# State-space build moved from the first feed-forward into the mixing stage, and that feed-forward's up products as seven block products

## The reference, cut to what matters

```python
# first block, token mixer: the mixing stage
y_hy = hyena_branch(hy_cols, p) @ p['hy_proj']                  # 512 -> 1024
g_hy, g_rw = jnp.split(jax.nn.sigmoid(gate_cols), 2, axis=-1)   # gate_cols = h @ w_in[:, gates], 1024 -> 2048
mixed = (g_hy * y_hy + g_rw * (y_rw @ p['rw_proj'])) @ p['w_out']

# second block, feed-forward (run twice, layers 0 and 1)
up = h @ w_up                                                   # 1024 -> 5632
up = causal_conv(up, conv_w, width=3) + conv_b
val, gate = jnp.split(up, 2, axis=-1)
y = (jax.nn.silu(gate) * val) @ w_down                          # 2816 -> 1024

# second block, S5 mixer, between the two feed-forwards
x[t] = A_bar * x[t-1] + B_bar @ u[t];  y[t] = Re(C @ x[t]) + d * u[t]   # 64 groups, 64 complex states, 16 channels
```

## Time and profile before

| what | us |
|---|---|
| median of 3 runs | 3600.9 (3598.59 to 3601.1) |
| the profiled execution | 3596.73 |
| its span, first to last instruction | 3594.9 |
| TensorE busy in the span | 3275.0 (91%) |
| VectorE, ScalarE, GpSimd busy | 1454.7 (40%), 621.7 (17%), 8.5 (0%) |
| mixing, first to last product | 851.0 to 1017.8 |
| first feed-forward, up products, then down products | 2503.2 to 2808.4, to 2945.8 |
| second feed-forward, up products, then down products | 3189.3 to 3444.9, to 3583.1 |

### The profile page before, as it was taken

How to read it: one execution, slowest core, us unless ns; L and a number is a source line. 1 busy time by engine, 2 the same in 40 slices (tenths; PEclk the granted TensorE clock), 3 DMA queues, 4 the chain that set the end, 5 groups by cost and what they waited for, 6 DMA issues and landing times. The chain is left out here.

```text
span 3594.9 us, 49905 instructions
## 1 busy us (share of the span) xinstructions
PE 3275.0 (91%) x21661; PEld 1745.5 (49%) x21661; DVE 1454.7 (40%) x2603; ACT 621.7 (17%) x1237; POOL 8.5 (0%) x40
## 2 busy tenths in 40 slices
PE   6978899898997988898989899999999976999998
PEld 3557787444444333333333343455444434468853
DVE  2255666444013000000001135652666674157776
ACT  2033332110011000000000122151221003031200
POOL 0000000000000000000000000000000000000000
PEclk8989999899997999999999999999999997999999
DMA  6134435311226999999999821102333554222233
GB/s 237 58 105 164 166 130 183 114 59 47 82 77 269 430 430 430 430 431 427 426 425 430 368 75 47 61 10 65 135 129 130 169 179 188 71 70 71 94 135 129
DMA packets 202974, 689.83 MB, mean 192 GB/s; under 512 B 31240, under 2 KB 96252, under 8 KB 176517
## 3 DMA queue, kind: packets, MB, share of 16 engines
q1 hardware_dynamic: 201768, 686.28, 49.1%
q10 hardware_dynamic: 989, 0.36, 0.0%
HBM read 661.94 MB, written 22.31 MB: 190 GB/s over the span
## 5 line engine op out<-in xcount | busy, mean ns | idle before, releaser
L2086 PE MATMUL banks<-weight_ring,xe_T 128*64 128x512 f32 x1312 | 296.7, 599 | 41.2 <-DMA weight_ring<-in_exp_w 38.9
L2859 PE MATMUL banks<-h_T,weight_ring 128*128 128x512 f32 x704 | 306.5, 594 | 2.2 <-PEq L91 2.2
L2859 PEld LDWEIGHTS banks<-h_T,weight_ring 128*128 128x128 f32 x704 | 132.2, 190 | 163.2 <-issue 163.1
L2086 PEld LDWEIGHTS banks<-weight_ring,xe_T 128*64 128x64 f32 x1312 | 91.0, 137 | 234.3 <-issue 160.8
L2102 PE MATMUL banks<-weight_ring,hid_T 128*64 128x512 f32 x656 | 146.8, 596 | 10.6 <-DMA weight_ring<-in_exp_w 10.6
L2422 PE MATMUL banks<-h_T,weight_ring 128*128 128x512 f32 x320 | 142.1, 597 | 0.0
L2086 PE MATMUL banks<-h_T,xe_T 128*64 128x512 f32 x464 | 105.4, 596 | 18.2 <-DMA h_T<-in_exp_w 18.2
L1735 PE MATMUL banks<-h_T,weight_ring 128*128 128x512 f32 x256 | 112.9, 600 | 3.9 <-PEq L91 3.9
L3787 PE MATMUL banks<-weight_ring,h_T 128*128 128x512 f32 x256 | 112.9, 603 | 2.6 <-PEq L91 2.6
L3152 DVE SCALAR_TENSOR_TENSOR conv<-banks,cols,conv 128x511 f32<-128x511 f32 (+1 forms) x96 | 71.9, 749 | 100.5 <-ACT conv L2999 97.9
L2249 DVE TENSOR_TENSOR hid<-silu,banks 128x1024 f32<-128x1024 f32 x16 | 19.5, 1221 | 222.2 <-issue 179.4
(11 more groups left out here) (667 smaller groups left out, 5227.8 us busy)
## 6 DMA issues: line engine op xcount, KB each, us to landing
weight_ring<-in_exp_w SPq DMA_DIRECT2D x123, 2048.0 KB, 15.7
h_T<-in_exp_w SPq DMA_DIRECT2D x41, 2048.0 KB, 15.7
weight_ring<-in_ada_w SPq DMA_DIRECT2D x24, 2048.0 KB, 7.9
weight_ring<-in_ffn_w_up SPq DMA_DIRECT2D x44, 1024.0 KB, 7.2
weight_ring<-in_ffn_w_down SPq DMA_DIRECT2D x20, 2048.0 KB, 7.7
expert_out<-in_exp_w SPq DMA_DIRECT2D x19, 2048.0 KB, 19.4
weight_ring<-in_mod_w SPq DMA_DIRECT2D x12, 2048.0 KB, 8.4
spare<-in_exp_w SPq DMA_DIRECT2D x9, 2048.0 KB, 20.9
```

The costliest lines, as they stand in the source:

```text
L2086: mm = pe.matmul(k.ps[64 * half:64 * half + 64, 2 * c + b % 2, :], R.rows[:, e // 2 % 2, kt, (e % 2) * CAP:(e % 2 + 1) * CAP], w[:, r, 512 ...
L2859: mm = pe.matmul(k.ps[:, b + c, :], w[:, c, kt, m * P:m * P + P], hT[:, kt, :], start=kt == 0, stop=kt == 7)
```

## The change

`S5Build` is opened around `mix_branches` instead of `conv_ffn`. The mixing loop is cut into 24 slots of 8 matmuls (for each tile: one gate product, the other, both branch products), so that the build's pieces can stand after single slots; the gates take banks 0 to 3, the branch products banks 4 and 5 (one set instead of two), the build banks 6 and 7. A build step now has two slots; `dve_inputs` of step i stands one step further ahead, with two buffers for the input powers and for the fractions, and the wait for the stored tables has gone from `dve_inputs` to `dve_outputs`. The `used` count for the branch weights is now raised by VectorE. At the stage's end SP stores the taps as they are in a new DRAM tensor and waits for it; in the first feed-forward's up products `scatter_taps` scatters them from there, 8 DMAs after each of 8 chunks. The first feed-forward takes the form of the second.

```diff
+        self.s5_tap_rows = nc.dram_tensor("s5_tap_rows", (P, 8, P), F32, kind="Internal").ap()
...
-def mix_branches(k, hT, hy, rw, mixed):
+def mix_branches(k, hT, hy, rw, mixed, side):
 
     nc = k.nc
+    pair = k.ps[:, 6:8, :]
+
+    SLOTS_IN, STEPS = 3 * DT, 7
+    turn_at = {STEPS + 2 * i: i for i in range(8)}
+    taps_at = {STEPS + 2 * i + 1: i for i in range(8)}
+    gate_bank = lambda i: 2 * (i % 2)
+    loaded_by = (2, 2, 3, 4, 4, 5, 6, 6)
     with sbuf(nc, "gates", [P, 2, 2, L], F32) as gates, \
-            stage(nc, "products", "gated", "linked", "mixed_done") as (block, products, gated, linked, mixed_done):
+            stage(nc, "gate_products", "products", "gated", "linked", "mixed_done", *S5Build.SEMS) as \
+            (block, gate_products, products, gated, linked, mixed_done, *side_sems):
+        side.sem = dict(zip(S5Build.SEMS, side_sems))
+
         @block.sync
         def _(sync):
+            side.sync_start(sync)
+            k.ring.load_ahead(sync, 1)
+            side.sync_blank(sync)
+            for i in range(8):
+                k.ring.load_ahead(sync, loaded_by[i])
+                side.sync_store(sync, i)
             k.ring.load_ahead(sync, 8)
+            side.sync_end(sync)
 
         @block.tensor
         def _(pe):
-            for i in range(DT):
-                j, m, b = i // 2, i % 2, 4 * (i % 2)
-                if m == 0:
-                    k.ring.wait(pe, 2 * j)
+            for s in range(SLOTS_IN):
+                i, part = s // 3, s % 3
+                j, m = i // 2, i % 2
                 wg = k.ring.chunk(2 * j).rearrange("p (c k n) -> p c k n", c=2, k=8)
                 wp = k.ring.chunk(2 * j + 1)[:, 0:2048].rearrange("p (c k n) -> p c k n", c=2, k=4)
-                if i >= 2:
-                    pe.wait_ge(mixed_done, i - 1)
-                for c in range(2):
+                if part < 2:
+                    if m == 0 and part == 0:
+                        k.ring.wait(pe, 2 * j)
+                    if i >= 2 and part == 0:
+                        pe.wait_ge(gated, i - 1)
                     for kt in range(8):
-                        mm = pe.matmul(k.ps[:, b + c, :], wg[:, c, kt, m * P:m * P + P], hT[:, kt, 0:L], start=kt == 0, stop=kt == 7)
-                if m:
-                    mm.then_inc(k.ring.used, 1)
+                        mm = pe.matmul(k.ps[:, gate_bank(i) + part, :], wg[:, part, kt, m * P:m * P + P], hT[:, kt, 0:L], start=kt == 0, stop=kt == 7)
+                    if part:
+                        mm.then_inc(gate_products, 1)
                 else:
-                    k.ring.wait(pe, 2 * j + 1)
-                for c, src in ((0, hy), (1, rw)):
-                    for kt in range(4):
-                        mm = pe.matmul(k.ps[:, b + 2 + c, :], wp[:, c, kt, m * P:m * P + P], src[:, kt, :],
-                                       start=kt == 0, stop=kt == 3)
-                mm.then_inc(products, 1)
+                    if m == 0:
+                        k.ring.wait(pe, 2 * j + 1)
+                    if i:
+                        pe.wait_ge(mixed_done, i)
+                    for c, left in ((0, hy), (1, rw)):
+                        for kt in range(4):
+                            mm = pe.matmul(k.ps[:, 4 + c, :], wp[:, c, kt, m * P:m * P + P], left[:, kt, :], start=kt == 0, stop=kt == 3)
+                    mm.then_inc(products, 1)
+                if s == 2:
+                    side.pe_c(pe, pair)
+                if s == 3:
+                    side.pe_cols(pe, pair)
+                if s in turn_at:
+                    side.pe_turn(pe, turn_at[s], pair)
+                if s in taps_at:
+                    side.pe_taps(pe, taps_at[s], pair)
...
         def _(act):
-            for i in range(DT):
-                act.wait_ge(products, i + 1)
-                if i % 2:
-                    act.sem_inc(k.ring.used, 1)
-                if i >= 2:
-                    act.wait_ge(mixed_done, i - 1)
-                b = 4 * (i % 2)
-                act.activation(gates[:, i % 2, :, :], k.ps[:, b:b + 2, :], ACT.Sigmoid).then_inc(gated, 1)
+            for s in range(SLOTS_IN):
+                i, part = s // 3, s % 3
+                if part == 1:
+                    act.wait_ge(gate_products, i + 1)
+                    if i % 2:
+                        act.sem_inc(k.ring.used, 1)
+                    if i >= 2:
+                        act.wait_ge(mixed_done, i - 1)
+                    act.activation(gates[:, i % 2, :, :], k.ps[:, gate_bank(i):gate_bank(i) + 2, :], ACT.Sigmoid).then_inc(gated, 1)
+                if s == 1:
+                    side.act_exp(act)
+                if s == 2:
+                    side.act_c(act, pair)
+                    side.act_waves(act)
+                if s in turn_at:
+                    side.act_step(act, turn_at[s], pair)
...
+            link, side_link = Chain(dve, linked), Chain(dve, side.sem["side_linked"])
+            side.dve_blank(dve)
+
+            def gate(i):
                 dve.wait_ge(gated, i + 1)
-                g, b = gates[:, i % 2, :, :], 4 * (i % 2)
-                link(dve.tensor_tensor(g, g, k.ps[:, b + 2:b + 4, :], ALU.mult))
+                dve.wait_ge(products, i + 1)
+                if i % 2:
+                    dve.sem_inc(k.ring.used, 1)
+                g = gates[:, i % 2, :, :]
+                link(dve.tensor_tensor(g, g, k.ps[:, 4:6, :], ALU.mult))
                 dve.tensor_tensor(mixed[:, i, :], g[:, 0, :], g[:, 1, :], ALU.add).then_inc(mixed_done, 1)
+
+            for s in range(SLOTS_IN):
+                if s and s % 3 == 0:
+                    gate(s // 3 - 1)
+                if s == 1:
+                    side.dve_angles(dve, side_link)
+                if s == 2:
+                    side.dve_factors(dve, side_link)
+                if s == 4:
+                    side.dve_columns(dve, side_link, pair)
+                    side.dve_powers(dve, side_link)
+                    side.dve_inputs(dve, side_link, 0)
+                if s == 6:
+                    side.dve_inputs(dve, side_link, 1)
+                if s in turn_at:
+                    if turn_at[s]:
+                        side.dve_taps(dve, turn_at[s] - 1, pair)
+                    side.dve_outputs(dve, side_link, turn_at[s])
+                if s in taps_at and taps_at[s] + 2 < 8:
+                    side.dve_inputs(dve, side_link, taps_at[s] + 2)
+            side.dve_taps(dve, 7, pair)
+            gate(DT - 1)
...
-                    mix_branches(k, k.hT, hy, rw, mixed)
+                    with ExitStack() as c3:
+                        mix_branches(k, k.hT, hy, rw, mixed, S5Build(k, c3))
...
-def conv_ffn(k, hT, layer, side):
+def conv_ffn(k, hT, layer, steps_follow):
...
+    units = [(j, c) for j in range(1, FF_M) for c in range(2)]
+    plain = 2
...
+                if steps_follow:
+                    sync.wait_ge(k.s5_blanked, 16 * 4)
                 for j in range(11):
                     k.ring.load_ahead(sync, j + 1)
-                    if side and j == 1:
-                        side.sync_blank(sync)
-                    if side and 2 <= j < 10:
-                        side.sync_store(sync, j - 2)
-                if side:
-                    side.sync_end(sync)
+                    if steps_follow and 1 <= j < 9:
+                        scatter_taps(k, sync, j - 1)
...
                         pe.wait_ge(joined, JOINS * (u - 1) + 4)
+                    else:
+                        pe.wait_ge(conved, 1)
                     block_sum(u, 5, wsum[:, 0], hsum[:, 0])
...
-        conv_ffn(k, k.hT, 0, S5Build(k, ctx))
+    conv_ffn(k, k.hT, 0, True)
...
-        self.inP, self.inT = work[:, 0:2, :], work[:, 2:4, :]
+        self.inP, self.inT = (work[:, 0:2, :], sb("s5_in_powers", [P, 2, n])[:]), work[:, 2:4, :]
-        self.f = sb("s5_fraction", [P, m])
+        self.f = (sb("s5_fraction", [P, m]), sb("s5_fraction_odd", [P, m]))
...
+        sync.wait_ge(self.sem["taps_copied"], 16)
+        sync.dma_start(self.k.s5_tap_rows, self.taps[:]).then_inc(self.sem["taps_kept"], 16)
+        sync.wait_ge(self.sem["taps_kept"], 16)
         for name in ("cp_stored", "in_stored", "tab_stored"):
             sync.wait_ge(self.sem[name], 16 * 8)
...
+        act.activation(self.tab[:, 1, :], self.f[i % 2][:], ACT.Sin, scale=2 * PI_DOWN).then_inc(s["tabled"], 1)
+        act.activation(self.tab[:, 0, :], self.f[i % 2][:], ACT.Sin, scale=PI_DOWN).then_inc(s["half"], 1)
...
-        if i:
-            dve.wait_ge(s["tab_stored"], 16 * i)
-        w, f = self.w, self.f[:]
+        w, f = self.w, self.f[i % 2][:]
-        if i:
-            dve.wait_ge(s["sined"], i)
+        if i >= 2:
+            dve.wait_ge(s["sined"], i - 1)
...
-        if i:
-            dve.wait_ge(s["in_turned"], i)
-        else:
+        if i >= 2:
+            dve.wait_ge(s["in_turned"], i - 1)
+        elif i == 0:
...
             dve.wait_ge(s["cp_stored"], 16 * i)
```

(48 more changed lines are left out.)

98 lines of the change are left out of this document (13 added, 85 removed).

## The result

The changed kernel takes 3580.28 us (median of 4 runs, 3572.45 to 3583.03) beside 3601.0 for the kernel before in the same job (4 runs, 3598.59 to 3604.3). The ratio is 0.9939, with a 95% interval of 0.9926 to 0.9951: 0.6% faster, by 20.7 us. The profiled execution took 3578.23, span 3576.4. The forecast was 3577.0, and its two large terms came out; of the gain 3 us are missing by the medians and 5 us by the spans, and the part on why the prediction was right says where.

A forecast was written before the change was run, and what follows sets the result against it. TensorE's own instructions bound the touched stages, transfers the experts' stretch. Mixing +24.9 (15.4 + 3.2 + 6.3) and feed-forward -48.8 sum to -23.9, from the median 3600.9 to 3577.0 us; own range 3572 to 3582, overall 3567 to 3592.

The forecast's parts named there:

- The second feed-forward as the price of the first: First feed-forward takes the second's stretches: up products 255.6 in place of 305.2 us, down products +0.8, together -48.8.
- The check by pieces: First feed-forward's up products: build's pieces 15.4 us go, and one product in eight of 20 units, 34.5; together -49.9.
- Scatter from DRAM at nothing: First feed-forward's up products: SP's 8 DMAs after each of 8 chunks cost nothing, upper bound 16 us; rival's chance 0.08.
- TensorE's own work in mixing, +15.4: Mixing: the build's instructions come in, 1.04 and 0.68 us plus eight steps of transposes and taps at 1.7 each.
- The waits, 0.9 and 2.3, and none later: Mixing: TensorE waits 0.9 us for the factors and 2.3 for the first taps copied, once each, 3.2 together.
- What VectorE has in hand: Mixing: a build step costs VectorE 14.6 us and TensorE 15.5, so VectorE gains 0.9 a step.
- The rival with VectorE setting the pace: Mixing: 2 to 2.5 us more in a VectorE step makes TensorE wait 1.5 in each of seven, +10.5, 3587; chance 0.17.
- The build in series: Mixing: VectorE's outputs wait each time for a store behind a weight chunk, +69 us, 3646; chance 0.05.
- The sines: Mixing, steps 3 and 6: sines done 3.5 us after a sigmoid, VectorE wants them at 3: 0.5 of 0.9 in hand.
- The table load without a drain: Mixing, ScalarE: a table load costs 1.28 us without the skill's 1.38 drain, which would make the total up to 2 higher.
- The end, +6.3: End of mixing: the taps' store lands 9.2 us after the expert chunk's issue, gap 10.2 with the barrier, +6.3.
- the rival in which the store passes the chunk by itself: End of mixing: the taps' store passes the expert chunk, so the end costs 0.2 in place of 6.3 us, 3571; chance 0.10.

The follow-up runs named there:

- plain up products: Changed kernel with layer 0's up products through the plain loop again, build still in mixing: 3613.67 us, ratio 1.0038 to the kernel before.
- one buffer: Changed kernel with inputs made one step later (no lead) and one buffer each for input powers and fractions: 3576.32 us, ratio 0.9935 to the kernel before.
- four more products: Changed kernel with four more 128x512 VectorE products (2.9 us) in each build step's outputs: 3589.03 us, one run.
- store first: Changed kernel with the store of the taps issued ahead of the first expert chunk's load: 3571.4 us, ratio 0.9921 to the kernel before.
- two more products: Changed kernel with two more 128x512 VectorE products (1.45 us) in each build step's outputs: 3582.22 us, one run.

## Why the prediction was right

By its own steps:

- **The second feed-forward as the price of the first.** Held: 255.5 for 255.6. The check by pieces was off by 1.3 and 1.5 in opposite directions, which the plain up products showed.
- **Scatter from DRAM at nothing.** Held. The up products with it (255.5) take what those without it take, and TensorE waits for no DMA in them. The upper bound of 16 us had nothing for it. SP's issues of eight took 5.65 us where 5.9 was forecast:

```profile
2571.13 5.65 SPq L3557 DMA_DIRECT2D s_steps<-s_tap_rows  x8
```

- **TensorE's own work in mixing, +15.4.** Busy time went from 166.71 to 182.46, +15.75, for the 15.6 that it spent on the build in the old place. That the forecast's 15.4 is so near is in part luck (the wait and the tile, as above).
- **The waits, 0.9 and 2.3, and none later.** 0.6 and 2.5 at the places named, and 0.2 at `pe_taps(0)`, where the forecast had VectorE in time by 0.4. Laying out both engines' lists from one moment, with durations of the old place, gave the two waits to 0.3 us. VectorE was busy for 131.3 us and not for some 140; my figure took its steps by their length, which holds the short gaps between instructions.
- **What VectorE has in hand.** 1.1 us a step measured for 0.9. The rival with VectorE setting the pace was near for all that: with 2.9 us more in a step mixing grew by 11.2 us.
- **The build in series.** Out: VectorE waited for no store in the changed kernel, and with one buffer mixing took 182.9 us. ScalarE did wait for the stored tables, 16.8 us in three waits, which the forecast had not laid out; TensorE waited for nothing there:

```profile
ACT s_b L3355 <- DMA s_matrices<-s_b: 16.8, 3, 8.8
```

- **The sines.** Forecast 0.5 late of 0.9 in hand; VectorE waited for them twice, up to 3.3 us. This was a miss, at steps 3 and 6 as named. The sines came 3.5 us behind the start of the sigmoid, as laid out; but VectorE came for them 2.0 and 0.3 us behind it and not 3, being further ahead in its list. It is off the path: TensorE waited for nothing at these steps, and after the last step VectorE stood for 8.3 us until TensorE's taps came. In the changed kernel, these two of VectorE's waits:

```profile
DVE step_taps L3549 <- PE banks L3401: 8.3, 1, 8.3
DVE s_b L3544 <- ACT s_b L3358: 4.8, 2, 3.3
```

- **The table load without a drain.** Mixing has the load with the next activation behind it at once:

```profile
875.44 1.28 ACT L3340 ACT_TABLE_LOAD   x1
876.73 0.31 ACT L3340 ACTIVATE s_work<-s_work 32x128 f32<-32x128 f32 x1
```

  The Trainium skill ("ScalarE: Activation LUTs", "What ACT_TABLE_LOAD costs") has another 1.38 us of drain for a switch. This trace does not show it: the activation starts 0.01 after the load's end. The forecast said so of the kernel before too; the earlier trace rows have the load at 2535.80 but not the activation behind it, which is this one, 0.01 after the load's end as well:

```profile
2537.09 0.31 ACT L3348 ACTIVATE s_work<-s_work 32x128 f32<-32x128 f32 x1
```

- **The end, +6.3.** +6.6. The store landed 9.3 after the chunk's issue, for 9.2, and so behind the chunk, which landed 8.0 after it: the rival in which the store passes the chunk by itself is out. Moving it ahead took all of the 6.6 away.
- **What the sum did not have.** It came to -23.9; the span shows -18.5, the medians -20.7. Every term of it held to 0.5 us. Of the missing 5.4, its own terms make 0.7, and 4.7 lie in stages that it had at nothing: S5 +2.0, attention +1.9, `w_out` +1.0, experts +0.8, all else +0.1, less 1.1 ahead of mixing. For the first three the tables at the result show where it went: the same instructions kept TensorE busy for 2.0, 2.5 and 1.0 us longer, at a granted clock that is 0.01 to 0.02 lower. In attention 1.7 of the 1.9 us lie in its first 7 us. Before and after, at its start:

```profile
2051.80:2058.00 6.20, 6.20 (x15) 2.85 (x16) 0.44 (x2) 2.83 (x5) 0.00 (x0) 1.00 0.60 232
```

```profile
2078.20:2084.00 5.80, 5.78 (x10) 2.55 (x11) 0.00 (x0) 1.84 (x3) 0.00 (x0) 0.71 0.59 232
```

  The wait ahead of them was 2.1 us before and 2.4 after. The step that failed is the last one of the sum: it carried the differences of two stages to the whole as if all others stayed, and they moved by up to 2 us each with the clock. Of these, only the 1.0 in the `w_out` products has a cause in the change that an experiment took away (the 10.5 us gap: with gaps of 10.4 to 11.8 these products took 57.7 to 58.2, with one of 3.5 they took 57.2 as before, and with one of 3.2, behind which the clock stayed, 55.5). For attention, 378.4 to 378.7 in all eight kernels with the build in mixing and 376.7 in the one execution of the kernel before, it stays open whether the change or that one execution is the reason. S5, from the last down product to the next up product, gave 244.2 before and 246.2 after, and 243.5, 244.5 and five times 246.1 to 246.5 in the experiments, whose code is the same there. So the change alone does not set it, and what does stays open.

## What to carry over

When work is moved from one stage to another, count the instructions as moved and not as saved; the gain must come from what the move makes room for, here an eighth fewer products in a stage with VectorE free (33.0 us; the 25.7 paid in mixing and behind it stand against 16.7 that the build had cost in its old place). That the block products had no room beside the build follows from the banks that both use in the code; no run tries it. Before giving a helper engine a lead and second buffers, lay out both lists from one moment: here the lead put 7.2 us ahead of the first result that was waited for, and its stage was 2.9 us longer for it in the trace, too little for the runs to tell. And look at what the queue's last entries are in a stage: a small store that a barrier waits for belongs ahead of the next stage's large load; putting it there took 7 us off the gap.

## What the runs showed of the hardware

One TensorE wait of 2.5 us, at the same point of TensorE's instruction list, left the clock at 1.00 in two kernels (the changed one, and the one with four more products), while it was 0.89 in the 15 us around it in three others. There the 16 matmuls behind it took 8.73 us in place of 7.03 (plain up products, store first), or 8.35 with another 0.4 in the transposes ahead of them (two more products). A gap of 3.5 us at the end of mixing (store first) and one of 3.9 (the kernel before) were followed by a granted clock of 0.91 in the next 19.5 us, and one of 3.2 by 1.00. The price is some 1.7 us each time (8.73 - 7.03; 57.2 - 55.5 in the `w_out` products), in addition to the wait. No run here tells what decides it, so a difference of 1 or 2 us between two profiled executions may be this and not the change.
